# One core, two transformer blocks in split-precision matmuls: side work ahead of the weight splits, norm sums as one product

## The reference

```python
def rmsnorm(x, g):                       # before every stage; the sum is over 2048 features
    xf = x * rsqrt(mean(x * x) + 1e-5)
    return xf * g
def grouped_rmsnorm(x, g, n_groups):     # after the SSD: 4 groups of 512 features
    ...
def first_block(x, mem, ...):
    mem_n = rmsnorm(mem, mem_norm)
    h = h + hybrid_mixer(rmsnorm(h), ...)             # SSD with 32 heads, then grouped_rmsnorm
    h = h + memory_cross_attention(rmsnorm(h), mem_n) # 4 heads
    h = h + swiglu(rmsnorm(h), ...)
def second_block(x, ...):
    h = rmsnorm(x)
    y_a = diff_attention(...)            # 8 heads
    y_b = stick_breaking_attention(...)  # 8 heads, here 4 pairs
    y_c = chunk_band_attention(...)      # 8 heads, here 4 pairs
    x = x + concat(y_a, y_b, y_c) @ w_o
    x = x + conv_swiglu(rmsnorm(x))
```

## Time and profile before

| | us |
|---|---|
| median of 3 runs (2786.55 to 2788.6) | 2786.58 |
| the profiled execution, time | 2785.78 |
| its span, first to last instruction | 2784.0 |
| PE busy | 2749.0 (99%) |
| DVE busy | 1946.7 (70%) |
| ACT busy | 1289.3 (46%) |
| POOL busy | 86.6 (3%) |
| one split: on ACT (L819), on DVE (L1216) | 1.06, 1.23 |
| one residual addition on DVE (L1651, L1653) | 0.70 |
| change of ACT's table; the four exponentials of an SSD head pair | 1.28; 1.2 |
| normalising of one band pair on DVE (L1509, L1512) | 1.4 |
| waits of PE not in the rows below: at 1618 us for a gather (L1525); near the end for a square (L826) | 0.8; 2.2 |

### The profile page before, as it was taken

The page is one execution under the profiler, slowest core; times in us unless marked ns, Lnnn a source line. Parts: engine busy times, 40 slices in busy tenths (PEclk is TensorE's granted clock), DMA queues, the critical chain, the costliest instruction groups (busy, mean ns, idle before and its releaser), DMA issues.

```text
span 2784.0 us, 40021 instructions
## 1 busy us (share of the span) xinstructions
PE 2749.0 (99%) x16612; PEld 2423.5 (87%) x16612; DVE 1946.7 (70%) x2382; ACT 1289.3 (46%) x1650; POOL 86.6 (3%) x61
## 2 busy tenths in 40 slices
PE   8999999999999999999999999999999999999997
PEld 7888998888898888888888889888988888888886
DVE  7777778766768665666566776775777757765775
ACT  5444546754545443444344545554444433433444
POOL 1000000002001000000000110000100000000001
PEclk9999999999999999999999999999999999999999
DMA  6555554456555555555555554443555655555553
GB/s 241 183 187 185 175 172 158 145 164 212 177 167 186 194 191 190 185 195 190 189 188 192 181 182 154 153 155 122 174 174 182 202 184 181 188 190 188 184 188 122
DMA packets 138197, 499.14 MB, mean 179 GB/s; under 512 B 15248, under 2 KB 16280, under 8 KB 137888
## 3 DMA queue, kind: packets, MB, share of 16 engines
q1 hardware_dynamic: 136224, 491.67, 53.5%
q10 hardware_dynamic: 1792, 4.91, 0.5%
HBM read 494.41 MB, written 2.11 MB: 178 GB/s over the span
## 4 chain that ended last, share of the span: by engine, by line
PE 96%; DVE 3%; ACT 1%; issue 0%; DMA 0%; DVEq 0%; ACTq 0%
PE PS L477 95%; DVE wlo L1216 1%; ACT whi L819 1%; DVE XG L1416 0%; DVE XG L1653 0%; DMA XG<-in_x 0%; DVE AR L1525 0%; DVE AR L1226 0%; DVE XG L1199 0%; PE PS L560 0%; PE PS L716 0%; ACT AR L1069 0%; DVE XG L1651 0%; DVE H L1210 0%; PE PS L638 0%
## 5 line engine op out<-in xcount | busy, mean ns | idle before, releaser
L477 PE MATMUL PS<-H,whi 128*128 128x512 f32 (+1 forms) x5472 | 1798.0, 381 | 9.0 <-DVE wlo L1681 8.1
L1216 DVE TENSOR_TENSOR wlo<-raw,whi 128x1024 fp32r<-128x1024 f32 x929 | 1128.7, 1229 | 674.7 <-ACT whi L819 669.7
L477 PE MATMUL PS<-H,wlo 128*128 128x256 f32 x5072 | 1423.7, 281 | 0.0
L819 ACT ACTIVATE whi<-raw 128x1024 fp32r<-128x1024 f32 x929 | 969.8, 1057 | 979.2 <-PE PS L477 958.3
L477 PEld LDWEIGHTS PS<-H,whi 128*128 128x128 f32 x5472 | 1002.3, 188 | 220.8 <-DVE H L1210 8.0
L477 PEld LDWEIGHTS PS<-H,wlo 128*128 128x128 f32 x5072 | 960.9, 189 | 2.0 <-issue 1.7
L477 PE MATMUL PS<-Y,whi 128*128 128x512 f32 (+1 forms) x2240 | 724.2, 378 | 1.1 <-DVE XG L1653 0.8
L477 PE MATMUL PS<-Y,wlo 128*128 128x256 f32 x2048 | 575.0, 281 | 0.0
L477 PEld LDWEIGHTS PS<-Y,whi 128*128 128x128 f32 x2240 | 408.3, 188 | 85.0 <-DVE XG L1653 2.0
L477 PEld LDWEIGHTS PS<-Y,wlo 128*128 128x128 f32 x2048 | 388.2, 190 | 0.2
L1525 DVE TENSOR_REDUCE AR<-PS 128x512 f32<-128x1024 f32 x140 | 171.5, 1225 | 14.9 <-PE PS L477 0.5
(11 more groups left out here) (168 smaller groups left out, 914.5 us busy)
## 6 DMA issues: line engine op xcount, KB each, us to landing
raw<-in_ffn SPq DMA_DIRECT2D x528, 512.0 KB, 4.3
raw<-in_w_in SPq DMA_DIRECT2D x177, 512.0 KB, 4.6
raw<-in_w_qkv SPq DMA_DIRECT2D x96, 512.0 KB, 3.8
raw<-in_w_out SPq DMA_DIRECT2D x64, 512.0 KB, 4.2
raw<-in_w_o SPq DMA_DIRECT2D x40, 512.0 KB, 3.8
raw<-in_w_q SPq DMA_DIRECT2D x8, 512.0 KB, 3.9
raw<-in_w_k SPq DMA_DIRECT2D x8, 512.0 KB, 3.9
raw<-in_w_v SPq DMA_DIRECT2D x8, 512.0 KB, 4.1
```

The costliest lines, as they stand in the source:

```text
L477: return e.matmul(out, l, r, start=start, stop=stop)
L819: a.then_inc(e.activation(c.whi[:, s % NW, :], c.raw[:, s % NRAW, :], ACT.Copy), "whi")
L1216: v.then_inc(e.tensor_tensor(c.wlo[:, s % NW, :], c.raw[:, s % NRAW, :], c.whi[:, s % NW, :].bitcast(F32), ALU.subtract), "wlo")
```

## The change

Seven edits, of which the first four belong together.

1. On ACT and on DVE `side.step(t)` goes from the end of the slot to its start, ahead of `split`, `leave` and `follow`. PE and POOL keep their order.
2. SSD head pairs start two slots later, stick-breaking and band pairs 0 to 3 slots later, so the last band pair ends two slots later.
3. `norm` and `mnorm`: the two products of 256 columns are one of 512 whose halves land apart; DVE adds them in `mean2` (one instruction more). `norm(6)`, the last, stays as it was.
4. The one-column products, and the second Newton chain on 2 columns with its ACT roots, are gone from `mnorm`, `norm(3)` and `norm(4)`. Instead two new pieces, `mcol` and `rcol`, turn a ready row into a column by two one-column products with the identity and a copy on DVE.
5. `grp`: POOL adds the two squared halves (512 wide), then the two 256-wide parts of that, and PE makes one product of 256 columns where it made four. PE's step is one slot later, those of ACT and DVE two.
6. The bank table follows from the new starts.
7. The value tiles wait for `mcol_ok` and `rcol_ok`.

```diff
 def tasks():
-    out += [(z + 2 + 4 * i, "ssd", i) for i in range(16)]
+    out += [(z + 4 + 4 * i, "ssd", i) for i in range(16)]
...
-    out += [(first_slot("wo2") + 14, "msq", 0), (first_slot("wo2") + 32, "mnorm", 0)]
+    out += [..., (first_slot("wo2") + 38, "mcol", 0)]
...
-    out += [(v + s, "stk", i) for i, s in enumerate((57, 71, 85, 99))]
-    out += [(v + s, "bnd", i) for i, s in enumerate((105, 114, 124, 136))]
+    out += [(v + s, "stk", i) for i, s in enumerate((57, 72, 87, 102))]
+    out += [(v + s, "bnd", i) for i, s in enumerate((108, 117, 127, 138))]
...
 # tensor_program
-    def norm_mm(bank, s, start, stop, cols):
-        mm(bank[:, 0:T], c.ones, s[:, 0:T], start, False)
-        last = mm(bank[:, 0:T], c.ones, s[:, T:2 * T], False, stop)
-        if cols:
-            for i in range(2):
-                o = bank[:, T + i:T + i + 1]
-                mm(o, s[:, i * P:(i + 1) * P], c.ones[:, 0:1], True, False)
-                last = mm(o, s[:, T + i * P:T + (i + 1) * P], c.ones[:, 0:1], False, True)
-        return last
+    def column(kind, i, row, ready, n, name):
+        bank = take(kind, i, "b")
+        p.wait_ge(ready, n)
+        mm(bank[:, 0:1], row[:, 0:P], c.ident[:, 0:1], True, True)
+        p.then_inc(mm(bank[:, 1:2], row[:, P:T], c.ident[:, 0:1], True, True), name)
...
     def norm(n):
-        last = norm_mm(bank, c.SUM, True, n != 6, n in (3, 4))
+        if n < 6:
+            last = mm(bank, c.ones, c.SUM, True, True)
...
     def grp(g):
-        yield from idle(4)
+        yield from idle(5)
         bank = take("grp", g, "b")
-        p.wait_ge("grp_sq", g + 1)
-        for n in range(4):
-            last = mm(bank[:, 0:T], c.ones, c.grp_q[n // 2][:, (n % 2) * T:(n % 2 + 1) * T], n == 0, n == 3)
-        p.then_inc(last, "grp_sum")
+        p.wait_ge("grp_add", g + 1)
+        p.then_inc(mm(bank[:, 0:T], c.ones, c.grp_q[0][:, 0:T], True, True), "grp_sum")
...
 # vector_program
+    def mean2(m, bank, eps, name):
+        v.then_inc(e.tensor_scalar(m, bank[:, 0:T], 1.0 / 2048, eps, ALU.mult, ALU.add))
+        v.wait_ge(*v.at)
+        v.then_inc(e.scalar_tensor_tensor(m, bank[:, T:2 * T], 1.0 / 2048, m, ALU.mult, ALU.add), name)
...
 # scalar_program and vector_program
     for t in range(N_SLOT):
+        side.step(t)
         if t % 2:
             split(t // 2 + NW)
         for stage, j in leave_at.get(t, ()):
             leave(stage, j)
...
-        side.step(t)
...
 # gpsimd_program
+    def grp(k):
+        q0, q1 = c.grp_q
+        yield
+        g.wait_ge("grp_sq", k + 1)
+        g.then_inc(e.tensor_tensor(q0, q0, q1, ALU.add))
+        g.wait_ge(*g.at)
+        g.then_inc(e.tensor_tensor(q0[:, 0:T], q0[:, 0:T], q0[:, T:2 * T], ALU.add), "grp_add")
+        yield
```

More of the change, by code:

```diff
@@ L179, in tasks @@
     a = first_slot("qa")
-    out += [(a + 4, "norm", 3), (a + 6, "mid", 0), (a + 28, "norm", 4), (a + 32, "qa", 0)]
+    out += [(a + 4, "norm", 3), (a + 6, "mid", 0), (a + 28, "norm", 4), (a + 32, "qa", 0), (a + 35, "rcol", 0)]
     v = after("ka")
@@ L216 @@
     "mnorm": [("b", 0, 2, "mnorm_mean", 1, 1)],
+    "mcol": [("b", 0, 2, "mcol_ok", 1, 1)],
+    "rcol": [("b", 0, 2, "rcol_ok", 1, 1)],
     "sc": [("b", 6, 7, "sc_root", 1, 1)],
@@ L500, in norm, with mcol, rcol @@
         p.wait_ge("sum_add", 7 * n + (6 if n == 6 else 7))
-        last = norm_mm(bank, c.SUM, True, n != 6, n in (3, 4))
-        if n == 6:
+        if n < 6:
+            last = mm(bank, c.ones, c.SUM, True, True)
+        else:
+            mm(bank[:, 0:T], c.ones, c.SUM[:, 0:T], True, False)
+            mm(bank[:, 0:T], c.ones, c.SUM[:, T:2 * T], False, False)
             yield from idle(3)
             p.wait_ge("sq", 8 * n + 8)
-            last = norm_mm(bank, c.SQ[1], False, True, False)
+            mm(bank[:, 0:T], c.ones, c.SQ[1][:, 0:T], False, False)
+            last = mm(bank[:, 0:T], c.ones, c.SQ[1][:, T:2 * T], False, True)
         p.then_inc(last, "norm_sum")
+        yield
+    def mcol(_):
+        column("mcol", 0, c.RMB, "mnorm_ok", 1, "mcol_turn")
+        yield
+    def rcol(_):
+        column("rcol", 0, c.RN, "rr", 1, "rcol_turn")
         yield
@@ L737, in done @@
         return f"acc{b}", n + 1
-    side = Side({"norm": norm, "mnorm": mnorm, "sc": sc, "cb": cb, "dt": dt, "xs": xs, "ssd": ssd, "grp": grp, "xa": xa,
-                 "dfa": dfa, "dfb": dfb, "stk": stk, "bnd": bnd})
+    side = Side({"norm": norm, "mnorm": mnorm, "mcol": mcol, "rcol": rcol, "sc": sc, "cb": cb, "dt": dt, "xs": xs, "ssd": ssd,
+                 "grp": grp, "xa": xa, "dfa": dfa, "dfb": dfb, "stk": stk, "bnd": bnd})
     b = 0
@@ L938, in grp @@
                 a.then_inc(e.activation(c.grp_q[n], z, ACT.Square))
-        yield from idle(4)
+        yield from idle(6)
         a.wait_ge("grp_sum", g + 1)
@@ L1345, in grp @@
         r = c.grp_q[0][:, 0:T]
-        yield from idle(6)
+        yield from idle(8)
         for n in range(2):
@@ L1421, in mid, with mcol, rcol @@
         v.wait_ge("norm_ok", 5)
-        v.then_inc(e.tensor_tensor(c.RN, c.RN, c.RN2, ALU.mult))
-        v.then_inc(e.tensor_tensor(c.ucol, c.ucol, c.ucol2, ALU.mult), "rr")
+        v.then_inc(e.tensor_tensor(c.RN, c.RN, c.RN2, ALU.mult), "rr")
+        yield
+    def mcol(_):
+        yield
+        v.wait_ge("mcol_turn", 1)
+        v.then_inc(e.tensor_copy(c.mcol, c.bank("mcol", 0, "b")[:, 0:2]), "mcol_ok")
+        yield
+    def rcol(_):
+        yield
+        v.wait_ge("rcol_turn", 1)
+        v.then_inc(e.tensor_copy(c.ucol, c.bank("rcol", 0, "b")[:, 0:2]), "rcol_ok")
         yield
@@ L1670, in cr @@
         yield
-    side = Side({"norm": norm, "mnorm": mnorm, "mem": mem, "sc": sc, "dt": dt, "ssd": ssd, "grp": grp, "xa": xa, "const": const,
-                 "cr": cr, "qa": qa, "mid": mid, "dfa": dfa, "dfb": dfb, "stk": stk, "bnd": bnd})
+    side = Side({"norm": norm, "mnorm": mnorm, "mcol": mcol, "rcol": rcol, "mem": mem, "sc": sc, "dt": dt, "ssd": ssd, "grp": grp,
+                 "xa": xa, "const": const, "cr": cr, "qa": qa, "mid": mid, "dfa": dfa, "dfb": dfb, "stk": stk, "bnd": bnd})
     def lo0(k):
```

44 lines of the change are left out of this document (19 added, 25 removed).

## The result

The changed kernel takes 2765.1 us (median of six runs, 2756.0 to 2773.5) against 2786.8 beside it (six runs, 2785.2 to 2788.6): a ratio of 0.991 [0.989, 0.994], 21.7 us less. I had said 2769.5, 17 us less. The direction was right, and so were the waits that went. The size was not: the time moved by something that stands nowhere in my prediction, and without it the change is worth 9 to 10 us.

A forecast was written before the change was run, and what follows sets the result against it. PE, busy 2749.0 of 2784.0 us, was taken as the bound; 7.0 us of products plus 10.1 of waits, 17.1 off 2785.8, gave 2768.7, and 2769.5 as median. Own range 2766 to 2774; 8 in 10, 2764.5 to 2779.

The forecast's parts named there:

- the second sentence on prices: PE's regular stream: one weight block, a `whi` and a `wlo` product, takes 0.36 us start to start, taken as 0.35.
- The products, 7.0 us: PE work saved: 5.2 us in four SSD groups, net 1.8 us from one-column products moved to `mcol` and `rcol`.
- The waits of `dif_y`, `bnd_w` with its restart, and L1095, 9.8 us: PE waits said to go: `dif_y` 1.8, `bnd_w` 3.4, restart and slow clock after it 1.9, value tiles (L1095) 2.7.
- L804, 0.3: PE's 1.1 us wait for the SiLU ahead of the last xs transposes was to shrink by 0.3 us.
- I put all of it between 0 and 5 us and take 0: Cost of side work holding splits and leaving tiles, said to be covered by splits leading PE by four sub-blocks, 11 us.
- POOL's group sums costing PE nothing: Eight more POOL instructions may cost DVE 8 us over four SSD groups, but this does not reach PE.
- Slower by the SSD's side work holding the splits: Rival, chance 0.05: head pairs at 450 to 572 us hold DVE's splits, PE loses 25 us, 2794.5 us.
- Waits back elsewhere: Rival, chance 0.17: removed waits return at other places, PE keeps only the 7.0 us from products, 2779.6 us.
- More goes than counted: Rival, chance 0.10: unpriced restarts, the rest of L804, the gather and the value tiles' other wait give 5 us more, 2764.5.

The follow-up runs named there:

- The products alone: The changed kernel's products, with the in-slot order and the starts of the kernel before; 2765.3 us, ratio 0.991.
- the order alone: The kernel before with side work ahead of the splits and the new starts, all products as they were; 2780.7 us, ratio 0.998.
- both with throwaway products: The kernel before plus an unread product 12 slots into each feed-forward: 512 columns wide 2775.0 us, 256 columns wide 2773.9 us.
- the one with `norm` 5 late: The kernel before with norm(5) summed by one product of 512 columns and placed one slot later; 2774.9 us, ratio 0.996.
- the old order in the first 40 slots: The changed kernel with that order kept there and norm(2) and norm(5) each one slot later; 2753.4 us, ratio 0.988.
- the 512-column product alone: The kernel before with norm(5) summed by one product of 512 columns instead of two of 256; 2787.2 us, ratio 0.997.
- `norm` 2 one slot later: The changed kernel with only norm(2), ahead of the first feed-forward, moved one slot later; 2758.5 us, ratio 0.987.
- the changed kernel again: The changed kernel rerun in another job with no edit; 2765.0 us, ratio 0.989.

## Why the prediction was wrong, and what of it was right

**The step that failed** is the second sentence on prices: that in the regular stream one weight block goes from start to start in 0.36 us, "I take 0.35". Rows 4 show 1771.12 - 1770.76 = 0.36, and 0.35 lies between two values, 346.7 and 353.3 ns, that PE holds for hundreds of microseconds. As a term to subtract from around a side product the difference is nothing. As the price of 4224 blocks in the feed-forwards it is 28 us, more than all the rest of the change, and the prediction gave it no term: its sum takes for granted that the blocks outside the edits take the same time before and after. Had I divided each feed-forward of before by its sub-blocks I would have had 2.78 us in the first and 2.83 in the second, with the same work and no waits, and asked.

What it does to the result: between levels that have the same steps in the feed-forwards the change is worth about 14.5 us (medians 2772.9 to 2758.6, both short; 2786.8 to 2772.0, one long). That this lies near the 17.1 forecast is luck in part. With the steps equal everywhere 9 to 10.4 us are left: the products are worth 5.5, the waits 9.6, and the new order, which I had put at 0, costs 5 to 6. Some 3 us of the rest are short steps in the smaller stretches, which the prediction does not have either; the last 1 to 2 us I have not placed. The medians differ by 21.7 because before's six runs beside it were all of the level with one long stretch, and half of after's have none. In the changed kernel only two levels are seen, and in both its profiles the second feed-forward is the short one; the first is a matter of chance. The Trainium skill (TensorE: Matmul & The Clock Gate, section "Back-to-back issue gap") gives one sustained spacing of products for each width. By that rule there would be one level; this case's trace doesn't agree, with 3463 and 3398 products in 600 us of the same stream at the same granted clock.

**The products, 7.0 us: each price right, the sum 1.5 too high.** The prices are in the timelines above. At equal steps the changed kernel saves 3.9 in z to wo2, where the terms make 5.65 and one group waits 1.2 for POOL, and 1.6 in qa and ka, where they make 1.35. The products alone gave 9.0 between equal levels, more than computed, and their profile says why: z to wo2 and qa, ka have 59 fewer long sub-blocks than before, 3.1 us.

**The waits of `dif_y`, `bnd_w` with its restart, and L1095, 9.8 us: right**, 9.6 after and 9.7 with the order alone. The clock stays full at 1940. The waits were worth more in some runs: behind the one of 2.7 us at 1899 the clock fell in three of the six profiles that have the old order throughout (both with throwaway products and the one with `norm` 5 late, not the one I had read), and behind `dif_y`'s 1.8 in one, for 1.5 us each.

**L804, 0.3: wrong.** The wait is 1.1 as before.

**"I put all of it between 0 and 5 us and take 0": wrong, and at its upper bound.** At equal steps the order costs 3.2 to 4.6 us at the start in the three profiles of the table that have it throughout, and 1.5 in wq to wv: 4.8 to 6.1 together. At the start there is no lead to cover a hold: I had computed with four sub-blocks of splits ahead, and these are not there yet. ACT's timeline of the changed kernel shows the hold:

```profile
26.46 0.63 ACT L833 ACTIVATE AR<-XG 128x512 f32<-128x512 f32 x1 [1.60 <-POOL AR L1731]
27.00 1.04 ACT L826 ACTIVATE whi<-raw 128x1024 fp32r<-128x1024 f32 x1
...
29.34 0.63 ACT L833 ACTIVATE AR<-XG 128x512 f32<-128x512 f32 x1 [0.78 <-POOL AR L1731]
29.88 2.94 ACT L826 ACTIVATE whi<-raw 128x1024 fp32r<-128x1024 f32 x3
```

The squares (L833) wait for POOL's sums, now ahead of the splits (L826). Behind a late split the raw buffer is refilled late, and the chain of waits then goes through that transfer:

```profile
28.01 1.31 POOL AR L1731
...
29.88 1.05 ACT whi L826
30.95 1.68 DVE wlo L1220
...
35.24 5.36 DMA raw<-in_w_in
40.62 1.07 ACT whi L826
```

and PE stops for 2.57 us in front of the sum over the first `sc` tile, its clock falling after it:

```profile
58.51 1.52 PE L477 MATMUL PS<-AR 128*128 128x512 f32 x2 [2.57 <-ACT AR L878]
...
59.00:62.50 3.50, 3.50 (x11) 2.56 (x10) 3.00 (x6) 2.56 (x4) 0.00 (x0) 0.52 0.54 174
```

This is the fall that I had seen go at 1953, back at another place. It doesn't come each time. In the second profile of the same kernel the stop is longer and the clock stays full, and the start is 1.4 us shorter (288.9):

```profile
58.70 1.12 PE L477 MATMUL PS<-AR 128*128 128x512 f32 x2 [2.77 <-ACT AR L878]
...
59.20:62.70 3.50, 3.50 (x19) 2.84 (x18) 3.01 (x6) 3.47 (x5) 0.00 (x0) 1.00 0.56 165
```

With the old order in the first 40 slots the stop is 1.1 and there is no fall. In wq to wv the first loss is at `norm` 1, where PE waits for POOL's last sum of the squares:

```profile
751.30 1.10 PE L477 MATMUL PS<-AR 128*128 128x512 f32 x2 [0.86 <-POOL AR L1731]
```

Its sub-block takes 4.78 us for 3.99. Two sub-blocks at the memory attention, where PE now waits 0.3 for L1373, take 0.7 more together, and eleven more sub-blocks are long, 0.6. The kernel with the order alone has the same. Why that sum comes later with the new order I have not shown.

**POOL's group sums costing PE nothing: wrong by 1.2.** The last group's product comes too early for the sum:

```profile
603.13 0.28 PE L477 MATMUL PS<-Y,wlo 128*128 128x256 f32 x1
604.61 0.67 PE L477 MATMUL PS<-AR 128*128 128x256 f32 x2 [1.20 <-POOL AR L1758]
```

The sum is made on another engine in two steps behind the squares, and three of the four groups had room for it.

**The rivals.** Slower by the SSD's side work holding the splits: nothing of it, z to wo2 is shorter by what the products save. Waits back elsewhere: true of some 6 to 7 us at the start, in wq to wv and at one group, but the ones removed stayed away. More goes than counted: the median is where that rival had it, for a reason that I had not given it.

**Open.** Why PE's stream has two steps, and what inside it a side product changes. The trace shows how often, not why. A single product of 512 columns that PE reached at once, with the next `whi` less than 0.46 us behind it, stands 87 times in regular streams of the eleven profiles, 20 times behind a long stretch, and the short step followed each time. With a stop of 0.05 us inside it was short seven times in eight, and with longer stops it was the one or the other. For other forms a prompt start is not enough. A single product of 256 columns without a stop was followed by the long step in 20 of 51 cases (all in the stretch of the attention heads), and the four products of the last SSD group in the old form in all six. At `norm` 5 the changed kernel's rows (1.07, then 0.51 us to the `whi`) are those of the kernel with the 512-column product alone, and the first goes on short and the second long. The trace doesn't hold what tells them apart.

## What to carry to other kernels

Where a long stream is bound by one engine that never waits, divide its time by its steps in every stretch and every profile: equal work at unequal steps is time to be had, and it hides in a median that sits between levels. Do it in the small stretches too: here 3 us that looked like the change's work were steps. List all run times before taking a median, and compare level with level; here a kernel 6 to 8 us faster level by level had a ratio of 0.998. Moving side work ahead of what feeds the bottleneck paid at the attention heads, where the feed has a lead, and cost at the program's start, where it has none yet.

## What the runs showed of the hardware

- A steady stream of weight blocks (a product of 512 and one of 256 columns) ran at 346.7 or 353.3 ns a block, with no wait and the granted clock full, and kept its step for over 700 us. One side product (0.43 or 0.86 us) that waited for nothing, put into both feed-forwards, left the short one behind in every run, by their times (23 runs of two kernels, 2772.6 to 2776.8). For a product of 512 columns that held in all 87 places of the eleven profiles; for one of 256 in 31 of 51.
- Whether PE's clock fell after a stop did not go by the stop's length alone. At 58 us stops of 1.77 (the order alone), 2.29 (`norm` 2 one slot later) and 2.57 us (the changed kernel) were followed by a granted clock of 0.5, the level of 1.2 GHz, for some 3 us; a stop of 2.77 at the same place (the changed kernel again) was not. The stop of 2.7 us at 1899 had a fall behind it in three of six profiles. Stops of 1.0 to 1.5 us had none. One fall cost 1.5 us.
